# Rotary partner rows made by transfers and ScalarE copies instead of by matmuls, in a two-block transformer stack

## What is computed

```
def apply_rope(t, cos, sin):                     # even mixer: 16 heads of 64
    t1, t2 = tf[..., :HEAD_DIM // 2], tf[..., HEAD_DIM // 2:]
    return concatenate([t1 * c - t2 * s, t2 * c + t1 * s])

def apply_axial_rope(x, cos, sin):               # second mixer kind
    rot = lambda z: concatenate([-z[..., q:], z[..., :q]])
    x_rot = concatenate([rot(xr), rot(xc)])      # row half and column half apart
    return x * c + x_rot * s

qa = apply_axial_rope(rmsnorm(qa, q_norm_g), cos_a, sin_a)
ka = apply_axial_rope(rmsnorm(ka, k_norm_g), cos_a, sin_a)
q_rope = apply_axial_rope(q_rope, cos_b, sin_b)
k_rope = apply_axial_rope(kr, cos_b, sin_b)
```

## Time and profile before

| | us |
|---|---|
| median of 3 runs (3440.7 to 3442.33) | 3442.33 |
| the profiled execution | 3441.55 |
| its span in the trace | 3439.7 |
| PE busy | 3400.9 (99%) |
| DVE busy | 2087.8 (61%) |
| POOL busy | 1989.7 (58%) |
| ACT busy | 1530.3 (44%) |

### The profile page before, as it was taken

One profiled execution on the slowest core, in us unless ns is written; L12 is line 12 of the kernel. 1 busy time (PEld: TensorE's weight loads), 2 busy tenths in 40 slices (PEclk: granted clock), 3 DMA queues, 4 the chain that ended last, 5 costly groups with the idle time before them and its releaser, 6 DMA issues. The chain is left out here.

```text
span 3439.7 us, 46281 instructions
## 1 busy us (share of the span) xinstructions
PE 3400.9 (99%) x17572; PEld 2761.2 (80%) x17572; DVE 2087.8 (61%) x2990; ACT 1530.3 (44%) x2388; POOL 1989.7 (58%) x2338
## 2 busy tenths in 40 slices
PE   9999999999999999999999999999999999999999
PEld 8888868888888888748888887788788876888887
DVE  5556666655764468766645667326767575238667
ACT  4334454333533355675333537434444555335444
POOL 6555645555655658745665557554655665546564
PEclk9999999999999999999999999999999999999999
DMA  4223203233222322202332220123222210232321
GB/s 173 89 77 117 85 20 118 79 110 111 86 98 91 130 70 93 71 1 83 123 111 103 83 76 26 56 92 123 98 98 92 86 59 8 93 105 92 114 107 62
DMA packets 87726, 301.56 MB, mean 88 GB/s; under 512 B 9936, under 2 KB 14544, under 8 KB 87120
## 3 DMA queue, kind: packets, MB, share of 16 engines
q1 hardware_dynamic: 85392, 296.50, 24.4%
q10 hardware_dynamic: 2112, 2.10, 0.2%
HBM read 296.46 MB, written 2.10 MB: 87 GB/s over the span
## 5 line engine op out<-in xcount | busy, mean ns | idle before, releaser
L408 POOL TENSOR_TENSOR w_lo<-w_raw,w_hi 128x256 fp32r<-128x256 f32 x1754 | 1364.6, 812 | 1091.5 <-ACT w_hi L381 841.9
L419 PE MATMUL bank<-xh,w_hi 128*128 128x512 f32 x2544 | 997.8, 392 | 3.9 <-issue 1.5
L421 PE MATMUL bank<-xh,w_lo 128*128 128x512 f32 x2544 | 989.2, 389 | 0.0
L420 PE MATMUL bank<-xl,w_hi 128*128 128x512 f32 x2544 | 989.2, 389 | 0.0
L381 ACT ACTIVATE w_hi<-w_raw 128x1024 fp32r<-128x1024 f32 (+2 forms) x485 | 498.5, 1039 | 671.3 <-DMA w_raw<-in_ffn_up 269.3
L419 PEld LDWEIGHTS bank<-xh,w_hi 128*128 128x128 f32 x2544 | 478.1, 188 | 106.5 <-issue 4.6
L420 PEld LDWEIGHTS bank<-xl,w_hi 128*128 128x128 f32 x2544 | 478.2, 188 | 99.7 <-issue 2.4
L421 PEld LDWEIGHTS bank<-xh,w_lo 128*128 128x128 f32 x2544 | 478.0, 188 | 99.5
L408 POOL TENSOR_TENSOR extra_lo<-extra_raw,w_hi 128x256 fp32r<-128x256 f32 x264 | 229.8, 905 | 126.1 <-ACT w_hi L381 113.1
L1099 DVE TENSOR_TENSOR y_tok<-y_tok,bank 128x512 f32<-128x512 f32 x232 | 157.4, 685 | 223.1 <-PE bank L978 223.1
L1133 DVE TENSOR_TENSOR work<-bank,sqsum 128x512 f32<-128x512 f32 x88 | 60.7, 690 | 267.7 <-PE bank L421 267.7
(11 more groups left out here) (454 smaller groups left out, 6154.2 us busy)
## 6 DMA issues: line engine op xcount, KB each, us to landing
w_raw<-in_ffn_up SPq DMA_DIRECT2D x176, 512.0 KB, 3.5
w_raw<-in_b_ffn_up SPq DMA_DIRECT2D x64, 512.0 KB, 3.5
extra_raw<-in_ffn_down SPq DMA_DIRECT2D x52, 512.0 KB, 4.5
w_raw<-in_b_gates SPq DMA_DIRECT2D x48, 512.0 KB, 3.4
extra_raw<-in_b_ffn_down SPq DMA_DIRECT2D x40, 512.0 KB, 4.5
w_raw<-in_od_in SPq DMA_DIRECT2D x33, 512.0 KB, 3.5
w_raw<-in_b_in SPq DMA_DIRECT2D x24, 512.0 KB, 3.6
w_raw<-in_ffn_down SPq DMA_DIRECT2D x20, 512.0 KB, 3.4
```

The lines of the kernel that those rows point to most:

```text
L408: ins = pool.tensor_tensor(lo_of(g, part), raw_of(g, part), hi_of(g, part).bitcast(F32), ALU.subtract)
L419: pe.matmul(out, wh, hi, start=first, stop=False)
L420: pe.matmul(out, wh, lo, start=False, stop=False)
L421: return pe.matmul(out, wl, hi, start=False, stop=last)
```

## The change

In the second mixer kind the partner rows are moved by on-chip transfers on ACT's queue: four of 32 partitions each for a `rot`, eight of 16 partitions each for `rotkr` and `rotup`. The features of a head are put in another order in the weights, so that partners are 32 (or 16) partitions apart. In the even mixer ACT copies each bank in four blocks of 32 partitions straight to the partner rows. The sign now lies in the sine table. All rotation matmuls and their PSUM banks are gone, and DVE multiplies partner rows from SBUF by the sine.

```diff
+EVEN_TILES = [item for item in EVEN_ORDER if item[0] != "rot"]
@@ even_act
-                    act.activation(raw[:, i % 4, :], bank[(c.tiles + n) % ACCS][:], ACT.Copy).then_inc(raw_copied, 1)
+                    if i >= 6:
+                        act.wait_ge(rotated, i - 5)
+                    for to in range(4):
+                        at = to + 1 - 2 * (to % 2)
+                        ins = act.activation(partner[32 * to:32 * to + 32, i % 4, :],
+                                             bank[(c.tiles + n) % ACCS][32 * at:32 * at + 32, :], ACT.Copy)
+                    ins.then_inc(raw_copied, 1)
@@ even_pe
-                elif kind == "rot":
-                    pe.wait_ge(acc_drained, acc_free(tile))
-                    pe.wait_ge(raw_copied, c.at("raw") + i - 2 + 1)
-                    pe.wait_ge(tables_loaded, 48)
-                    pe.matmul(out, e_tab[:, 2432:2560], raw[:, i % 4, :], start=True, stop=True).then_inc(side_done, 1)
@@ even_dve
+                if kind == "rot":
+                    dve.wait_ge(raw_copied, c.at("raw") + i - 1)
+                    ch.link(dve.tensor_tensor(tmp[:, i % 2, :], partner[:, i % 4, :], e_tab[:, S:2 * S], ALU.mult))
+                    dve.tensor_tensor(e_qk[:, i - 2, :], e_qk[:, i - 2, :], tmp[:, i % 2, :], ALU.add)\
+                       .then_inc(rotated, 1)
@@ second mixer kind
-        STEPS2 = ("sum", "add")
+        STEPS2 = ("sum", "add", "rot", "rotkr", "rotup")
+        MOVE_AT = {("rot", 0): ("qk", 1), ("rot", 1): ("qk", 2), ("rot", 4): ("qk", 3), ("rot", 2): ("kr", 0), ("rotkr", 0): ("va", 0),
+                   ("rot", 3): ("va", 0), ("rotup", 0): ("upr", 1), ("rotup", 1): ("upn", 0)}
@@ mix2_pe
-                elif kind in ("rot", "rotkr", "rotup"):
...
-                    pe.matmul(out, turn, src, start=True, stop=True).then_inc(side_done, 1)
@@ mix2_act
+            def move(r):
+                src, made = rotated_tile(*ROTS2[r])
+                wide = HD // 2 if ROTS2[r][0] == "rot" else 16
+                act.wait_ge(acc_drained, drained(T + TILES2.index(made)))
+                if r >= 2:
+                    act.wait_ge(rotated, c.at("rotated") + r - 1)
+                for to in range(0, P, wide):
+                    at = to + wide if to // wide % 2 == 0 else to - wide
+                    act.dma_start(b_partner[to:to + wide, r % 2, :], src[at:at + wide, :]).then_inc(partner_moved[r % 2], 16)
-                if (kind, i) == ("rotup", 0):
+                if (kind, i) == ("upn", 1):
                     act.wait_ge(rotated, c.at("rotated") + ROTS2.index(("rot", 3)) + 1)
+                for r, item in enumerate(ROTS2):
+                    if MOVE_AT[item] == (kind, i):
+                        move(r)
@@ mix2_dve
+                if kind in ("rot", "rotkr", "rotup"):
+                    dve.wait_ge(partner_moved[r % 2], moves(L, r))
```

More of the change, by code:

```diff
@@ L214, in build @@
         pbuf = work[:].rearrange("p (g a) s -> p g a s", a=2)
-        raw = work[:, 2:6, :]
+        partner = work[:, 2:6, :]
         BF16 = mybir.dt.bfloat16
@@ L292, in build @@
         side_done, raw_copied, rotated = sem("side_done"), sem("raw_copied"), sem("rotated")
+        partner_moved = [sem(f"partner_moved{i}") for i in range(2)]
         tables_loaded, odd_loaded = sem("tables_loaded"), sem("odd_loaded")
@@ L1421, in even_end @@
             c.blocks += 20
-            c.tiles += len(EVEN_ORDER)
-            c.add("side", 12)
+            c.tiles += len(EVEN_TILES)
+            c.add("side", 4)
             c.add("raw", 8)
@@ L1431, in even_pe @@
             k.blocks = c.blocks + FIRST
-            for n, (kind, i) in list(enumerate(EVEN_ORDER))[FIRST:]:
+            for n, (kind, i) in list(enumerate(EVEN_TILES))[FIRST:]:
                 tile = c.tiles + n
@@ L1438, in even_pe @@
                     pe.wait_ge(acc_drained, acc_free(tile))
-                    pe.wait_ge(acc_drained, drained(c.tiles + EVEN_ORDER.index(("val", i))))
+                    pe.wait_ge(acc_drained, drained(c.tiles + EVEN_TILES.index(("val", i))))
                     for m in range(4):
@@ L1481, in even_act @@
             g = c.blocks
-            for n, (kind, i) in enumerate(EVEN_ORDER):
+            for n, (kind, i) in enumerate(EVEN_TILES):
                 if kind in ("lin", "val"):
@@ L1494, in even_act @@
             k = c.copy()
-            k.tiles += len(EVEN_ORDER)
+            k.tiles += len(EVEN_TILES)
             out_act(act, k, 1, c.blocks + 12, y)
@@ L1539, in even_dve @@
                         pools((i - 5) // 2)
[L1540 to L1548, removed]
                 elif kind == "grp":
@@ L1551, in even_dve @@
                     dve.wait_ge(side_done, side)
-                    dve.wait_ge(rotated, sum(k == "rot" for k, _ in EVEN_ORDER[:n]))
+                    dve.wait_ge(rotated, turns)
                     dve.tensor_scalar(tmp[:, i, :], src, e_small[:, i:i + 1], None, ALU.mult).then_inc(acc_drained, 1)
@@ L1566, in even_dve @@
                         constants()
-            dve.wait_ge(acc_drained, drained(c.tiles + len(EVEN_ORDER) - 1))
+            dve.wait_ge(acc_drained, drained(c.tiles + len(EVEN_TILES) - 1))
             dve.wait_ge(rotated, 8)
@@ L2146, in build, with moves, pieces @@
         ROTS2 = [item for item in ORDER2 if item[0] in ("rot", "rotkr", "rotup")]
+        MOVE_AT = {("rot", 0): ("qk", 1), ("rot", 1): ("qk", 2), ("rot", 4): ("qk", 3), ("rot", 2): ("kr", 0), ("rotkr", 0): ("va", 0),
+                   ("rot", 3): ("va", 0), ("rotup", 0): ("upr", 1), ("rotup", 1): ("upn", 0)}
+        def moves(layer, r):
+            def pieces(item):
+                return 4 if item[0] == "rot" else 8
+            return 16 * (layer * sum(map(pieces, ROTS2[r % 2::2])) + sum(map(pieces, ROTS2[r % 2:r + 1:2])))
         SIDES2 = 3 + 1
@@ L2534, in mix2_dve @@
                     dve.wait_ge(xl_ready, xn + j + 1)
[L2535 to L2548, removed]
                 elif kind in ("upr", "upn"):
@@ L2833, in even_table, with turn_sign, turned_order @@
     pool = np.concatenate([np.repeat(inv_count[0:2], HD, 0), np.repeat(inv_count[2:4], HD, 0)], 1)
[L2834 to L2840, removed]
-        low = (p - first) % width < width // 2
-        r[p + (width // 2 if low else -width // 2), p] = -1 if low else 1
-    return r
+    return np.concatenate([np.cos(ang), turn_sign(HD) * np.sin(ang), mask, pool], 1).astype(f)
+def turn_sign(width):
+    return np.where(np.arange(P) % width < width // 2, -1, 1)[:, None]
+def turned_order(dim):
+    return np.arange(dim).reshape(2, 2, dim // 4).transpose(1, 0, 2).reshape(-1)
 def second_table():
```

59 lines of the change are left out of this document (40 added, 19 removed).

## The result

The changed kernel takes 3452.41 us (median of 7 runs, 3450.02 to 3454.03), the kernel before 3442.26 beside it (3440.13 to 3443.65). The ratio is 1.0028, 95% interval 1.0018 to 1.0037: 10 us slower, where 7 us faster was forecast. The profiled execution took 3450.87, so it stands 9.3 over that of before.

What follows compares the result with a forecast made beforehand. The prediction took PE, busy 99% of the span, as the bound, with DVE close behind. Savings of 3.3 us (even mixer) and 3.8 (two layers) sum to 7.1: 3434.5 profiled, 3435.2 against the median, range 3430 to 3441.

Steps and rivals of the forecast that it cites:

- what a removed matmul is worth: PE, both stages: a rotation costs 0.85 to 0.87 us; eight make 7.0 us, all 24 would give 20.9.
- the even copies: Even mixer, ACT: a 32-partition copy costs 0.48 us, so a tile takes 2.05 us instead of 0.60.
- landing: Second kind: a transfer's rows land 2.3 us after the start of the last issue; a quiet store takes 1.8.
- the trains of 12, 8 and 8: Second kind, ACT's queue: late transfers for `rotkr` with `rot` 3, then `rotup` 0, then `rotup` 1, issued in a chain.
- the shorter table: Tables get shorter by the change; costed at nothing.
- The bank order: Second layer: one gate tile instead of two between the last attention units; costed at nothing, 1 to 2 us if cover fails.
- rival D: Just before the second kind's attention, PE idles and its clock falls to 1.2 GHz: 4.5 us more a layer, 3444; chance 0.06.
- From there DVE sets the pace: Even mixer, `lin` 7 to `val` 1: DVE's 21.8 us of work, not PE, sets the time; 3.3 us saved of 7.0.
- I take 0.48: Second kind, ACT's queue: each DMA issue holds it 0.48 us, taken from SP's small steady train; 1.9 us saved a layer.
- A: Second kind: issues cost 0.3 us or less, PE sets both layers' end, whole gain 17.3 us, about 3425; chance 0.12.
- B: Second kind: issues at 0.56 us and landing at 3.5 lose 1.5 a layer, a draw at 3442; chance 0.20.
- C: Second kind: loaded DMA engines slow the chain's 27 issues to a mean of 0.80 us, +10.2 us, 3452; chance 0.12.

Runs made afterwards that it cites:

- even_one: Even mixer as changed but one 128-partition ACT copy a tile instead of four, partner exchange left out; second kind as in the kernel before: 3441.52 us, ratio 1.0000.
- second_only: Second mixer kind as changed, with 44 transfers a layer on ACT's queue; even mixer as in the kernel before: 3449.61 us, ratio 1.0023 to before.
- even_filled2: Even mixer as changed, second kind as before, plus unused matmuls in PE's waits (11 ahead of `lin` 6, 18 ahead of the second transpose): 3440.80 us, ratio 1.0000.
- after_filled: The changed kernel plus unused matmuls in PE's waits, in the even mixer and in each second-kind layer: 3446.54 us, ratio 1.0012 to the kernel before.

## Why the prediction was wrong

The right parts: what a removed matmul is worth is borne out (in even_one PE reached the first transpose 6.9 us earlier, for 7.0); the even copies follow each other every 0.60, 2.40 a tile, where 0.48 and 2.05 were forecast; `lin` 6 began at 402.66 for 402.1; landing was 2.1 for 2.3; the trace shows the trains of 12, 8 and 8 and DVE idle for the DMA ahead of the last rotation. The start came 0.5 earlier, costed at nothing; since second_only, whose even table is that of before, has 388.03 at the first norm of the table, the shorter table is not shown to be the cause. The bank order cost nothing between the two kernels: PE's wait of 1.5 us in the second layer's gate tiles stands in both traces.

**Even mixer, -3.3 forecast, +4.5 in the trace.** Two terms failed.
- The clock, missing from this stage's sum. The prediction had it as rival D, at 0.06, at one place, and wrote that no row showed it. Rows of before did. Its windows, just behind a wait of 0.78 us:

```profile
2740.00:2745.00 5.00, 4.22 (x27) 3.71 (x26) 0.95 (x2) 2.83 (x5) 3.54 (x6) 0.96 0.27 79
2745.00:2750.00 5.00, 5.00 (x17) 3.97 (x16) 0.00 (x0) 0.12 (x1) 3.72 (x6) 0.70 0.00 0
```

  17 matmuls in 5 us. Over 50 us (2700 to 2750) this is 0.97, over 100 it is 0.98, which is easily passed over. In after the two waits cost 1.6 us at `lin` 6 and at least 2.0 from the second transpose to the first fillers of the attention (5.33 us from 445.23 to 450.56, before 3.34 from 443.35 to 446.69). even_filled2 shows it by taking the loss away. (`lin` 7's drain, 417.88 for 415.3, is late by this 1.6, by 0.6 of `lin` 6's start and by 0.35 of the copies.) The Trainium skill, TensorE: Matmul & The Clock Gate, Part 1, has the two levels and says that idleness brings the lower one; the traces agree, with 0.43 us between matmuls of 512 columns after a wait and 0.23 otherwise.
- "From there DVE sets the pace": right, but its work was mis-sized. From `lin` 7's drain to `val` 1's it took 26.5 us (417.88 to 444.40) for 23.9. Idle between were 2.8, so 23.7 of work; the same stretch before held 20.4 (26.5 less idle pieces of 1.34, 3.34 and two of 0.70; the prediction counted the two of 0.70 as work, 21.8). That is +3.3 where I had allowed 0.3. All eight sums now take 1.1 us (before, 0.69 to 1.21), and three small casts 0.65 instead of 0.23. The slower DVE goes with a busier POOL. In after, POOL stood still from 426.09 to 428.98 and from 436.24 to 437.91: the four DVE products with two SBUF sources that began in these pieces took 0.69 each, the six others between 429 and 444 took 1.1. The casts of 0.23 in before began while POOL stood still, those of 0.65 in after while it worked. One sum in before (429.05) took 0.69 although POOL worked, and no run took POOL's work away, so the cause is argued and not shown. The same 27 us in before and in after, POOL's busy time being the last of the five:

```profile
417.00:444.00 27.00, 26.54 (x113) 20.17 (x111) 20.17 (x28) 7.65 (x9) 18.99 (x22) 1.00 0.21 76
```
```profile
417.00:444.00 27.00, 22.62 (x99) 17.89 (x98) 22.74 (x27) 12.02 (x17) 22.43 (x26) 1.00 0.26 93
```

  The Trainium skill, SBUF — State Buffer, section "SBUF: two separate sides", says that a DVE operation with two SBUF inputs and a GpSimd operation that reads SBUF lock each other out of a shared port pair. The sine products got their second SBUF input by this change; that fits, with the same reservation, and it does not account for the casts, which have one.

**Second kind, -1.9 a layer forecast, +2.5 in the trace.** The step that failed is "I take 0.48" for the price of an issue; 0.64 was measured. By the first layer, less 3.88: the last `kn` copy ends at 76.6 instead of the forecast 72.0, 4.6 late. The 28 issues took 18.0 us; at 0.48 they would have taken 13.4, which is those 4.6. The other terms miss by under 1 us and cancel (moves begin 0.8 late, reciprocal to `upr` 0's copy 0.5 longer, the last stretch 0.8 shorter). I chose SP's small steady train over ACT's own queue; the row of ACT's four, 2.57, held the truth. In the second layer the attention starts only 1.1 us later than before, since the kernel before lost 1.6 there to the clock event just shown, and after then loses about 1.5 more at its own half clock (window 2812.5 to 2817.5).

**The rivals.** A is out. B (issues 0.56, landing 3.5) had the issue price nearly, and its layer loss of 1.5 is the nearest of all, though with a landing of 3.5 that was 2.1. C named 3452 but by a mean of 0.80 that was not there: 0.64 was measured, under its threshold of 0.74; the total agrees by accident. D's mechanism was right and its place too narrow: PE's idle time at the end of the first layer came as 2.50, 1.94 and 1.39 us ahead of `kn` 2, `kn` 3 and the attention, and what the clock cost lay mostly in the even mixer. The prediction's own sum gives 3443.8 at 0.64 an issue (it wrote 3445), so the price of the issues alone explains about half of the 17.3 us between forecast and result; the other half is the even mixer's 7.8. The range failed because each term was bounded within one stage, and none asked what a new wait of PE does to the matmuls behind it. By the runs 5.9 us, with intervals of 3, come back when the clock is kept (after_filled). The 4 that stay are ACT's copies and issues and DVE's slower work, less what the removed matmuls gave; these parts are not separated by a run.

## What to carry to other kernels

Price a DMA by its issues on the queue that gives it out, and lay data out so that one instruction does it. When a change turns steady PE work into waits of 2 us and more, add the half clock behind each wait, and look for it in the trace of before in windows of 5 us, not of 50. Taking matmuls from the busiest engine gives only the distance to the engine next in line, less what the new wait costs in clock: in even_one 6.9 us became 3.9 at DVE and 0.9 behind the clock.

## What the runs showed of the hardware

- ACT's queue takes 0.55 to 0.62 us for each SBUF to SBUF transfer by the median (single ones 0.47 to 1.5; in trains of eight 0.62 to 0.69 each), the same for 16 rows of 2 KB, 64 of 2 KB and 64 of 0.5 KB. Every second partition as source and destination costs the queue nothing more.
- A 32-partition copy of 512 columns from PSUM on ACT is no cheaper than one of 128 partitions, and a train of them goes on at 0.60 us each (eight in 4.81), where two of 128 took 1.08, 0.48 from the first to the second.
- The granted clock falls behind some waits of PE of only 0.8 us, and not behind others: at the same wait of 0.78 us for ACT's square, the first layer of before kept it (1.00 from 2015 to 2020) where the second lost 1.6 us. Runs of one kernel differ by it: of even_one's eleven the fastest (3436.13) had a mean of 0.999, the slowest (3445.14) 0.995.
